# Modulating the gathered expert rows on VectorE between weight pieces, and splitting the next weight piece ahead of two waits

## The reference

```python
def expert_choice_ffn(h, w_router, w_gate, w_up, w_down):
    xt = h.reshape(-1, shp[-1])
    cap = EC_FACTOR * xt.shape[0] // N_EXPERTS
    affin = jax.nn.softmax((xt @ w_router).astype(jnp.float32), axis=-1)
    gates, idx = lax.top_k(affin.T, cap)
    xs = xt[idx]
    hid = jax.nn.silu(jnp.einsum('ecd,edf->ecf', xs, w_gate)) * jnp.einsum('ecd,edf->ecf', xs, w_up)
    y = jnp.einsum('ecf,efd->ecd', hid, w_down) * gates[..., None].astype(xt.dtype)
    out = jnp.zeros_like(xt).at[idx.reshape(-1)].add(y.reshape(-1, shp[-1]))
    return out.reshape(shp)

        h = modulate(rmsnorm(xs, norm_ffn[l]), sh2, sc2)      # h * (1 + scale) + shift
        xs = xs + g2 * expert_choice_ffn(h, w_router[l], w_gate[l], w_up[l], w_down[l])
```

## Time and profile before

| | |
|---|---|
| median of 3 runs | 3839.99 us |
| the profiled execution's own time | 3818.11 us |
| its span in the trace | 3816.3 us |
| PE busy | 3390.0 us, 89% |
| DVE busy | 2207.6 us, 58% |
| ACT busy | 1765.1 us, 46% |
| POOL busy | 1028.8 us, 27% |
| HBM traffic | 203 GB/s over the span |

### The profile page before, as it was taken

One profiled execution on the slowest core, in us unless ns is written; L12 is line 12 of the kernel. 1 busy time (PEld: TensorE's weight loads), 2 busy tenths in 40 slices (PEclk: granted clock), 3 DMA queues, 4 the chain that ended last, 5 costly groups with the idle time before them and its releaser, 6 DMA issues.

```text
span 3816.3 us, 52395 instructions
## 1 busy us (share of the span) xinstructions
PE 3390.0 (89%) x21052; PEld 3049.4 (80%) x21052; DVE 2207.6 (58%) x2203; ACT 1765.1 (46%) x1916; POOL 1028.8 (27%) x717
## 2 busy tenths in 40 slices
PE   6899999997989998995859999999999999999991
PEld 4677777786668776874759999999999999999991
DVE  5643343453533354334857777777777777777774
ACT  5633433553532354223335555555555555555552
POOL 1064064012230022005151233332223333212331
PEclk9999999998999999987979999999999999999996
DMA  7755555674124312433558777777777777777766
GB/s 277 274 197 192 176 182 193 208 272 170 34 97 160 122 34 71 163 105 126 190 175 271 235 252 251 255 243 254 257 230 254 253 253 243 255 255 229 255 225 245
DMA packets 544952, 775.87 MB, mean 203 GB/s; under 512 B 16160, under 2 KB 409600, under 8 KB 536144
## 3 DMA queue, kind: packets, MB, share of 16 engines
q1 hardware_dynamic: 507072, 616.60, 47.9%
q0 software_dynamic: 37776, 157.84, 12.7%
HBM read 708.19 MB, written 66.19 MB: 203 GB/s over the span
## 4 chain that ended last, share of the span: by engine, by line
PE 55%; DVE 14%; issue 12%; ACT 10%; DMA 5%; POOL 4%; DVEq 0%; ACTq 0%; POOLq 0%
PE PS L787 15%; PE PS L571 11%; PE PS L743 10%; PE PS L789 6%; DVE lo_f L1421 6%; ACT hi_f L1071 5%; DVE wlo L1142 2%; PE PS L691 2%; ACT whi L861 1%; DMA arena_ab<-k_rope 1%; PE PS L662 1%; PE PS L710 1%; PE PS L518 1%; PE PS L665 1%; PE PS L678 1%
## 5 line engine op out<-in xcount | busy, mean ns | idle before, releaser
L1421 DVE TENSOR_TENSOR lo_f<-raw_f,hi_f 128x2048 fp32r<-128x2048 f32 x384 | 1016.3, 2667 | 372.4 <-ACT hi_f L1071 372.2
L787 PE MATMUL PS<-xT,hi_f 128*128 128x320 f32 x4096 | 1062.5, 347 | 4.8 <-DVE lo_f L1421 4.4
L789 PE MATMUL PS<-xT,lo_f 128*128 128x160 f32 x4096 | 966.1, 236 | 0.0
L1142 DVE TENSOR_TENSOR wlo<-raw,whi 128x2048 fp32r<-128x2048 f32 x204 | 474.1, 2342 | 658.7 <-ACT whi L861 658.3
L789 PEld LDWEIGHTS PS<-xT,lo_f 128*128 128x128 f32 x4096 | 782.4, 191 | 0.0
L787 PEld LDWEIGHTS PS<-xT,hi_f 128*128 128x128 f32 x4096 | 768.9, 188 | 11.7 <-DVE lo_f L1421 9.1
L1071 ACT ACTIVATE hi_f<-raw_f 128x2048 fp32r<-128x2048 f32 x384 | 723.7, 1905 | 26.3 <-PE PS L789 22.9
L861 ACT ACTIVATE whi<-raw 128x2048 fp32r<-128x2048 f32 x204 | 387.2, 1916 | 540.1 <-PE PS L743 302.7
L787 PE MATMUL PS<-hid,hi_f 128*128 128x320 f32 x2048 | 572.8, 363 | 62.1 <-DVE hid L1466 62.1
L789 PE MATMUL PS<-hid,lo_f 128*128 128x160 f32 x2048 | 498.4, 243 | 0.0
L787 PEld LDWEIGHTS PS<-hid,hi_f 128*128 128x128 f32 x2048 | 407.4, 199 | 65.1 <-DVE hid L1466 65.1
(11 more groups left out here) (278 smaller groups left out, 5089.7 us busy)
## 6 DMA issues: line engine op xcount, KB each, us to landing
raw_f<-w_gate SPq DMA_DIRECT2D x128, 1024.0 KB, 4.8
raw_f<-w_up SPq DMA_DIRECT2D x128, 1024.0 KB, 5.4
raw_f<-w_down SPq DMA_DIRECT2D x128, 1024.0 KB, 5.1
raw<-w_ada SPq DMA_DIRECT2D x96, 1024.0 KB, 5.1
raw<-w_in SPq DMA_DIRECT2D x60, 1024.0 KB, 5.4
raw<-w_out SPq DMA_DIRECT2D x48, 1024.0 KB, 5.0
arena_ab<-x_sample POOLq DMA_DIRECT2D x8, 1024.0 KB, 12.2
arena_cd<-x_sample POOLq DMA_DIRECT2D x8, 1024.0 KB, 6.1
```

What stands on the lines that cost most here:

```text
L787: nc.tensor.matmul(PS[:, b + m, 0:2 * CAP], hi_f[:, n % NSPL_F, r, w], x, start=(kt == 0), stop=False, skip_group_check=True)
L789: ins = nc.tensor.matmul(PS[:, b + m, 0:CAP], lo_f[:, n % NSPL_F, r, w], x[:, 0:CAP], start=False, stop=(kt == last_kt), skip_group_check= ...
L1142: nc.vector.tensor_tensor(wlos[slot(n)], raws[slot(n)], whis[slot(n)].bitcast(F32), ALU.subtract).then_inc(lo_ok, 1)
L1421: nc.vector.tensor_tensor(lo_f[:, n % NSPL_F], raw_f[:, n % NRAW_F], hi_f[:, n % NSPL_F].bitcast(F32), ALU.subtract).then_inc(f_lo_ok, 1)
```

## The change

The six POOL instructions of `modulate` go. In their place DVE does the same arithmetic in five blocks of 512 columns, one for the context rows and four for the latent rows, two instructions each: a `scalar_tensor_tensor` (row times reciprocal root times table) and an addition. In the loop the five blocks stand at steps n = 4, 6, 8, 10 and 12, ahead of that step's split, and the first and second wait for the gathers there. For the first expert they stand ahead of the loop. The table `a2` is also made by DVE, by two instructions, no longer by POOL's four. PE waits for each block apart, no longer for all of the rows at once. Ahead of the loop DVE's four splits are spread: the first before the blocks, the other three between the `take_lo` steps.

Besides, ACT and DVE do the split of piece n + 4 ahead of some waits: ACT at n = 4q + 1 before it waits for `gsum`, and at n = 4q + 3 (but not at 15) before it waits for `hraw`; DVE at n = 4q + 3 (but not at 15) between `hraw` and the remainder of `hid`.

```diff
@@ PE @@
             pe.wait_ge(affT_ok, 2)
-            pe.wait_ge(h_in, 1)
             for j in range(4):
+                pe.wait_ge(h_in, j + 2)
                 if j:
                     pe.wait_ge(x_lo, j)
                 turn_tokens(j)
@@
-                    if cc == 0:
-                        pe.wait_ge(h_in, e + 2)
                     if cc == 3:
                         turn_outputs(2)
+                    pe.wait_ge(h_in, e * 5 + 7 + cc)
                     pe.wait_ge(x_lo, e * 4 + 4 + cc)
                     turn_tokens(cc)
@@ ACT, expert_hi @@
                     if n < 16 and n % 4 == 1:
                         nc.scalar.activation(part[:, 0, :]..., PS[:, 0:2, CAP:2 * CAP], ACT.Copy).then_inc(part_ok, 1)
+                        split_f(n + NSPL_F, e)
                         act.wait_ge(gsum_ok, e * 4 + n // 4 + 1)
                         nc.scalar.activation(hg[:], gsum[:], ACT.Silu).then_inc(silu_ok, 1)
                     if n < 16 and n % 4 == 3:
                         nc.scalar.activation(part[:, 1, :]..., PS[:, 2:4, CAP:2 * CAP], ACT.Copy).then_inc(part_ok, 1)
+                        if n < 15:
+                            split_f(n + NSPL_F, e)
                         act.wait_ge(hid_ok, e * 4 + n // 4 + 1)
...
+                    if n < 15 and n % 2:
+                        continue
@@ DVE @@
+            def modulate(j, arrived, before):
+                if j == 0:
+                    g, r, a, s = g_p[:, 0:DQ], g_p[:, DQ:DQ + 1], a2_p[:], s2_p[:]
+                    dve.wait_ge(gp_in, arrived)
+                else:
+                    c = slice((j - 1) * CC, j * CC)
+                    g, r, a, s = g_s[:, c], g_s[:, D:D + 1], a2_s[:, c], s2_s[:, c]
+                    dve.wait_ge(gs_in, arrived)
+                nc.vector.scalar_tensor_tensor(out=g, in0=g, scalar=r, in1=a, op0=ALU.mult, op1=ALU.mult).then_inc(h_mid, 1)
+                dve.wait_ge(h_mid, before + j + 1)
+                nc.vector.tensor_tensor(g, g, s, ALU.add).then_inc(h_in, 1)
             xh = [0]
-            for n in range(NSPL_F):
-                split_f(n, 0)
+            dve.wait_ge(tab_in, 16 * (3 + 3 * Q))
+            link(nc.vector.scalar_tensor_tensor(out=a2_p[:], in0=a2_p[:], scalar=1.0, in1=y_p[:], op0=ALU.add, op1=ALU.mult))
+            link(nc.vector.scalar_tensor_tensor(out=a2_s[:], in0=a2_s[:], scalar=1.0, in1=y_s[:], op0=ALU.add, op1=ALU.mult))
+            split_f(0, 0)
+            for j in range(5):
+                modulate(j, 16, 0)
             for j in range(4):
                 take_lo(j)
+                if j < 3:
+                    split_f(j + 1, 0)
@@ DVE, expert_lo @@
                         nc.vector.tensor_tensor(hraw[:], hg[:], usum[:], ALU.mult).then_inc(hid_ok, 1)
+                        if n < 15:
+                            split_f(n + NSPL_F, e)
                         dve.wait_ge(hid_hi, e * 4 + n // 4 + 1)
...
+                    if n in (4, 6, 8, 10, 12):
+                        modulate(n // 2 - 2, e * 16 + 32, e * 5 + 5)
+                    if n < 15 and n % 4 == 3:
+                        continue
                     if n + NSPL_F < PIECES_E:
                         split_f(n + NSPL_F, e)
@@ POOL @@
-                pool.wait_ge(tab_in, 16 * (3 + 3 * Q))
-                for a, y in ((a2_s, y_s), (a2_p, y_p)):
-                    link(nc.gpsimd.tensor_scalar(a[:], a[:], 1.0, None, ALU.add))
-                    link(nc.gpsimd.tensor_tensor(a[:], a[:], y[:], ALU.mult))
...
-            def modulate(n, mid):
...
             gather()
-            modulate(16, 2)
             nc.gpsimd.nop().then_inc(y_free, 1)
             with pool.Fori(0, NE) as e:
...
                 gather()
-                modulate(e * 16 + 32, e * 2 + 4)
                 pool.wait_ge(ic_ok, e + 1)
```

More of the change, by code:

```diff
@@ L1757, in gather @@
                                              in_offset=bass.IndirectOffsetOnAxis(ap=ig_p[:, 0:1], axis=0)).then_inc(gp_in, 16)
-            def modulate(n, mid):
[L1760 to L1763, removed]
-                nc.gpsimd.tensor_scalar(g_p[:, 0:DQ], g_p[:, 0:DQ], g_p[:, DQ:DQ + 1], None, ALU.mult).then_inc(h_mid, 1)
-                pool.wait_ge(h_mid, mid - 1)
-                nc.gpsimd.nop().then_inc(turn, 1)
-                nc.gpsimd.tensor_tensor(g_s[:, 0:D], g_s[:, 0:D], a2_s[:], ALU.mult)
-                nc.gpsimd.tensor_tensor(g_p[:, 0:DQ], g_p[:, 0:DQ], a2_p[:], ALU.mult).then_inc(h_mid, 1)
-                pool.wait_ge(h_mid, mid)
-                nc.gpsimd.nop().then_inc(turn, 1)
-                nc.gpsimd.tensor_tensor(g_s[:, 0:D], g_s[:, 0:D], s2_s[:], ALU.add)
-                nc.gpsimd.tensor_tensor(g_p[:, 0:DQ], g_p[:, 0:DQ], s2_p[:], ALU.add).then_inc(h_in, 1)
             gather()
-            modulate(16, 2)
             nc.gpsimd.nop().then_inc(y_free, 1)
```

## The result

The changed kernel takes 3687.28 us, the median of 4 runs (3681.62 to 3703.31), beside 3834.91 us (3828.17 to 3848.72) for the kernel before on the same chip: a ratio of 0.9617, with a 95% interval of 0.9573 to 0.9662. The forecast was 3721 with a range from 3693 to 3785. The direction and the place were right, the time lies 5.7 us under the range. The profiled executions went from 3818.11 to 3681.82 us, 136.3 less, where the sum said 119.0.

A forecast was written before the change was run, and what follows sets the result against it. PE was taken to bound the expert loop, stopped by waits and clock. Gains of 14.0 + 2.0 + 62.1 + 40.9 = 119.0 us, off a median of 3840, gave 3721 us, range 3693 to 3785.

The forecast's parts named there:

- The stop at `hid`: First down piece, before the last two k-tiles: PE's wait for the remainder of `hid` goes, all 62.1 us.
- The margin of 1.3 us: At the end of `hid`: done at 2691.0, PE coming at 2692.3, so no stop.
- Its cause: DVE late at `hid`: six splits lengthened beside POOL's modulation lose 9 us, 3793 ns in the mean against 2291 elsewhere.
- Rivals 1 and 2: Gather's landing stalls PE at piece 8 (3749 or 3790 us, chance 0.08); part of `hid` stop stays (3770 us, 0.12).
- Rival 3: Splits stay long without POOL's arithmetic and the `hid` stop stays; only 16 us ahead of the loop won, 3824; chance 0.04.
- Rival 4: Slower: the first block's wait moves PE's stop from `hid` to piece 8 and lengthens it; 3886 us, chance 0.04.
- The clock: Behind the `hid` stops the lower clock level (1.2 GHz) goes: 3.1 or 1.7 us a time, 40.9 us in all.
- The sign "scatters near 105 us apart": Interval between scatters in the expert loop: 111.6 us in the mean before, less 4.0 and 2.7.
- Ahead of the loop: From the gather's landing to PE's first expert matmul: five DVE blocks replace POOL's modulation, gain 14.0 us.
- the table instructions: Output projection: POOL's table instructions lengthen a split beside them to 4.27 us, not 2.29; gain 2.0 us.
- The gather's second half: In the loop: its issue on POOL is slowed beside a DVE split, so it lands 0.8 us later.
- the margin at piece 8: `gsum` of step 5 done at 2654.5 against PE's need at 2655.6: 1.1 us, no stall.

The follow-up runs named there:

- e2: Changed kernel without the splits ahead of waits: the five blocks on DVE, the old order; 3821.05 us, ratio 0.9983.
- e9: Kernel before with only ACT's splits moved ahead of its two waits; 3731.82 us, ratio 0.9733.
- e1: Kernel before with ACT and DVE splitting ahead of their waits, POOL still modulating; 3713.12 us, ratio 0.9708.
- e3: Kernel before with POOL's modulation in the loop left out, gathered rows unmodulated from the second expert on; 3706.56 us, ratio 0.9685.
- the second set: Changed kernel run again with no edit, on another chip than the first reading; 3693.44 us, ratio 0.966.
- e8: Changed kernel with blocks at steps 6 to 14 and PE's first piece of the next expert ahead of its last output transposes; 3687.21 us, ratio 0.9628.
- e10: e8 with PE's loop over the experts written out 16 times; 3670.8 us, ratio 0.9604.
- e5: Changed kernel with all five blocks at step n = 4; 3778.99 us, ratio 0.9862.

## Why the prediction missed the time and met the mechanism

**The stop at `hid`: right.** All 62.1 us are gone. The end of `hid` was worked out as 2691.0, 65.9 us behind the scatter, and that is what it is. The margin of 1.3 us is not right: it was taken to PE's 67.2 us in the kernel before, where PE was late itself. PE now comes at 66.4, and 0.5 us are left. A block takes 746 + 692 ns less the overlap, 1.4 us as taken, the splits 2289 ns, the first block's wait 5.24 us for the 5 forecast.

**Its cause: half right.** The prediction saw one cause, six long splits that lose 9 us, and used the split-ahead order as a given. The runs show two cures, each of which alone takes the stop away or all but 0.2 us of it, and they don't add. Times behind the scatter at which PE comes to the last part of `hid` and at which that part is done (one expert of each trace), and time per expert:

| | PE comes | `hid` done | per expert |
|---|---|---|---|
| before | 67.2 | 71.1 | 111.62 |
| blocks on DVE, old order (e2) | 67.3 | 72.7 | 112.62 |
| ACT's order alone (e9) | 67.0 | 67.8 | 105.57 |
| order alone (e1) | 66.4 | 66.6 | 104.42 |
| no modulation in the loop (e3) | 66.4 | 65.9 | 104.07 |
| both parts (changed) | 66.4 | 65.9 | 104.07 |

The time of an expert follows DVE's lateness and then stands at a floor. Rivals 1 and 2 left no wait in the changed kernel. Rival 3 (splits stay long) is out by the splits of e2, e3 and the changed kernel. Rival 4, slower, is nearest to e2: without the new order the modulation on DVE gives the loop nothing and takes 1.0 us per expert.

**The clock: right.** The granted clock is 1.00 through the loop (0.97 before). Each of the 12,928 matmuls of the loop has its counterpart in the changed kernel. Counted from start to start, those of pieces 16 and 17, where the stop and the slow stretch lie, take 102.4 us less over the 16 experts; stop and clock were forecast at 62.1 + 40.9 = 103.0.

**The step that failed: DVE's lateness was priced at one place only.** The prediction says that PE has one large wait in the loop and prices what DVE's lateness does there, at `hid`, and the clock behind it; what the same lateness does to PE ahead of that place, at the splits of pieces 13 to 15, stands in no term of the sum. The loop and the first expert gave 116.6 us, not 103.0: 113.4 in the fifteen intervals and 3.2 in the first expert (111.44 to 108.21 from its first matmul to its scatter). In the kernel before, the waits have these two rows as well, which the prediction left out:

```profile
PEld PS L787 <- DVE lo_f L1421: 9.1, 23, 0.8
...
PE PS L787 <- DVE lo_f L1421: 4.4, 17, 0.6
```

The same comparison, matmul by matmul, says where and how much: the matmuls of pieces 12 to 15 take 13.8 us less in the changed kernel, nearly all of it at or just behind the first matmul of pieces 13, 14 and 15, in every expert but the first. That closes the gap of 13.6 us: 102.4 + 13.8 = 116.2 of 116.6. The rows show less than that, since they list only part of these short waits and not the slower start behind them. The cause is that DVE runs behind PE, by whatever makes it late: the waits are there in the kernel before, with long splits, and in e2, with short ones and more work (15.7 us, some of it for `hraw`), and they are gone in e1, where the splits are long but ordered anew, in e3 and in the changed kernel. In e9 they are 6.4 of the 22.5 us that its fifteen intervals lose to the floor; the other 16.1 are at its 0.8 us stops.

The prediction's own rows held the sign: piece 15 was to end at 2688.5, and six k-tiles more (3.1 us) are 2691.6, but PE came at 2692.3. The sign "scatters near 105 us apart" carried the same error: 104.07.

**Ahead of the loop: the step right, its neighbour too small.** From the gather's issue to the first expert matmul it was 39.1 us and is 25.1: 14.0, as forecast. The gather's issue itself came 6.0 us earlier (1916.18 to 1910.15), where 2.0 were taken for the table instructions. All of that arises at one place. Compared matmul by matmul, the kernel before is 0.7 us ahead of the changed one at 1800 us and 7.0 us behind it at 1810, at the split of the earlier trace rows:

```profile
1807.67 1.91 ACT L861 ACTIVATE whi<-raw 128x2048 fp32r<-128x2048 f32 x1 [10.79 <-DMA raw<-w_out]
1814.01 0.79 PE L743 MATMUL PS<-whi,ahi 128*128 128x512 f32 x1 [7.04 <-DVE wlo L1142]
```

The raw weights landed late, so ACT's rounded part started 3.6 us later than in the changed kernel (1804.08); the split beside POOL's table instructions took 2.0 us longer; and behind PE's stop of 7.04 us the granted clock was 0.50 from 1814 to 1818, where the changed kernel, with a stop of 0.76 us, had 1.00. Some of the 7.7 us came back later. Long splits at this place go with the tables on POOL; of e3:

```profile
1811.36 3.53 DVE L1142 TENSOR_TENSOR wlo<-raw,whi 128x2048 fp32r<-128x2048 f32 x1
```

The longest is 3.5 to 4.5 us in the four kernels with the tables on POOL, and 2.29 in all the others. Whether the late landing belongs to the change too is open: it shows in the kernel before and in e9 (waits of 10.8 and 9.3 us for it, and PE stops of 7.0 and 6.3), but e1 and e3, which have the tables on POOL as well, wait 6.7 and 5.5 us there, about the 6.5 of the changed kernel. And the issue of the gather varies over all profiled executions, from 1910 to 1937 with the tables on POOL and from 1910 to 1923 with them on DVE. The sum then closes: 119.0 + 13.6 + 4.0 - 0.3 at the end of the kernel = 136.3.

**The gather's second half: cost there, harmless.** I added 0.8 us for an issue slowed beside a DVE split. POOL's timeline:

```profile
2563.75 2.78 POOL L1795 DMA_INDIRECT resid_s<-y_s,ic_s  x1 [84.57 <-DVE y_p L1470]
2579.35 1.00 POOL L1779 DMA_INDIRECT g_s<-h_s,ig_s  x1 [10.94 <-issue]
2580.66 2.59 POOL L1781 DMA_INDIRECT g_p<-h_q,ig_p  x1 [0.30 <-issue]
```

The issue takes 2.59 us for the 0.98 of the earlier trace rows, and yet the first block starts 24.28 us behind the scatter, where POOL started 24.25 behind it. The landing isn't later; that is the 0.8 us of the 1.1 us by which the margin at piece 8 was set too small.

**The two rules of the Trainium skill.** For the half rate of a scalar_tensor_tensor ("Vector Engine (DVE) Microarchitecture Reference", "Points that are easy to get wrong") the new row again doesn't agree: 746 ns for 512 columns with two SBUF inputs, beside 692 for the addition. For "SBUF — State Buffer", "SBUF: two separate sides", by which the gather's issue need not be slowed, the 2.59 us show an issue that is slowed, but a landing that isn't.

**The base.** The forecast missed the median by 33.7 us (3721 - 3687.28). Of these 17.3 are the sum's (136.3 - 119.0). The other 16.4 are the base: I took the saving off a median that stood 21.9 us above its profiled execution, and the median of the changed kernel stands 5.5 above its own. Either half alone would have left the time inside the range. The median of the kernel before was 3834.91 us with one run more, and 3827.60, 3832.31 and 3819.24 in the later sets, 5 to 21 us under the base. As ratios the forecast was 3721 / 3840 = 0.969, the results 0.9617, 0.966: the second set lies within 0.3% of it, less than the two sets differ.

## What to carry to other kernels

When one engine's queue makes the bound engine stop, write down how late it comes to that place and how late the bound engine does; two cures of one lateness don't add, and each change should be priced alone and together. Moving work onto an engine that has room as a total can cancel itself: short splits gave 9 us, the added blocks and the wait for their data took more, and only a reordering of two engines that waited for each other in turn made it pay. When an engine is late at one place, look for what it costs ahead of that place too: here waits too short to stand out, on the bound engine, came to 13.8 us.

## What the runs showed of the hardware

- A PE that reaches the branch of its loop without having waited stood 3.3 to 3.9 us behind it in 6 of 15 passes (e8), with the lower clock behind. With a 1.1 us wait ahead of the branch it never did (all other looped kernels), and with the loop written out it never did (e10). What PE waits for there is not shown; the place and the cure are.
- Beside POOL's arithmetic a 128x320 subtraction of DVE took 4.92 us in e1, not 0.49, and two splits 4.8 us each. The loss is not in proportion to the columns: 4.4 us there, 2.5 us a split.
- Stops of about 3.6 us brought 3.4 us of the 1.2 GHz level in most experts of e5, stops of 5.2 to 5.4 us brought 6.8 us of it in e2, and neither the 0.8 us stops of e9 nor the 2.56 us stop in the first expert of the kernel before brought any.
